# Ending two middle units in phase one, and loading the query weights by pairs of heads on the activation queue

## The reference, cut to what matters

```
p  = rms_norm(x) @ w_in              # 1024 x 2304: q, k, v of two attentions
h  = x + [rms_norm(stick_breaking(q,k,v)), rms_norm(sink_window(q,k,v))] @ w_out
xn = rms_norm(h)
q  = xn @ w_q                        # 1024 x 2048: 8 heads x 2 halves x 128
s1, s2 = q[:,:,0] @ keys_1.T, q[:,:,1] @ keys_2.T
idx, gate = top 16 of the sums of the top 16 of s1 and of s2; gate = softmax
y  = h + sum over 8 heads x 16 experts of gate * gelu(u[idx] . xn) * v[idx]
out = rms_norm(y)
```

## Time and profile before

| | |
|---|---|
| median of three runs | 3066.2 us |
| the profiled execution | 3064.77 us, its span 3063.0 us |
| mean granted TensorE clock | 0.91 of full speed |
| TensorE busy | 2455.0 us (80%) |
| VectorE busy | 2209.8 us (72%) |
| POOL busy | 1530.8 us (50%) |
| ScalarE busy | 1413.2 us (46%) |
| moved by DMA | 1216.86 MB, mean 397 GB/s |
| of it the gathers' queue | 1108.81 MB |

### The profile page before, as it was taken

One profiled execution on the slowest core, in us unless ns is written; L12 is line 12 of the kernel. 1 busy time (PEld: TensorE's weight loads), 2 busy tenths in 40 slices (PEclk: granted clock), 3 DMA queues, 4 the chain that ended last, 5 costly groups with the idle time before them and its releaser, 6 DMA issues.

```text
span 3063.0 us, 44243 instructions
## 1 busy us (share of the span) xinstructions
PE 2455.0 (80%) x13294; PEld 1144.1 (37%) x13294; DVE 2209.8 (72%) x5717; ACT 1413.2 (46%) x3303; POOL 1530.8 (50%) x1597
## 2 busy tenths in 40 slices
PE   7978778787768888878788888888778877778777
PEld 4755334343323332433243323333343334432222
DVE  3278647894667867886788768886878767786886
ACT  2235324652246533753376337753676345643233
POOL 0045444454445555555645565555545555455554
PEclk8999989899879999999989998999999987899989
DMA  8379999999999999999999999999999999999997
GB/s 337 98 281 393 423 394 416 402 404 379 424 419 414 419 418 422 415 408 406 424 419 415 402 416 421 411 409 415 422 414 417 392 420 423 420 402 417 426 422 311
DMA packets 243631, 1216.86 MB, mean 397 GB/s; under 512 B 30528, under 2 KB 90304, under 8 KB 107200
## 3 DMA queue, kind: packets, MB, share of 16 engines
q0 software_dynamic: 152528, 1108.81, 87.4%
q1 hardware_dynamic: 67968, 91.78, 8.4%
q10 hardware_dynamic: 22896, 13.44, 1.4%
HBM read 1197.56 MB, written 16.47 MB: 396 GB/s over the span
## 4 chain that ended last, share of the span: by engine, by line
DMA 34%; PE 24%; DVE 21%; issue 8%; DVEq 5%; ACT 3%; ACTq 1%; POOL 1%; SPq 0%; POOLq 0%
DMA r_uv<-peer_uv,f_idx 31%; DVE r_uv L1222 8%; PE f_y_acc L1769 6%; PE f_z L1654 5%; PE f_q_ps L1695 3%; PE f_y_acc L1750 2%; PE f_y_acc L1621 2%; DMA f_work<-w_out 1%; POOL r_uv L1000 1%; PE f_o_sw L1681 1%; PE f_z L1512 1%; PE f_o_sw L1621 1%; DVE f_ind L1363 1%; ACT f_diag L1146 1%; ACTq L1144 1%
## 5 line engine op out<-in xcount | busy, mean ns | idle before, releaser
L1000 POOL DMA_INDIRECT r_uv<-peer_uv,f_idx x1056 | 1278.5, 1211 | 1188.8 <-PE f_y_acc L1769 818.6
L1222 DVE CUSTOM_DVE_ANT_0 r_uv<-r_uv,r_x_rep 128x1024 f32<-128x1024 f32 x1056 | 1289.4, 1227 | 555.9 <-DMA r_uv<-peer_uv,f_idx 547.5
L1769 PE MATMUL f_y_acc<-r_uv,f_diag 128*32 128x512 f32 x4224 | 678.6, 662 | 330.0 <-ACT f_diag L1146 329.4
L1140 ACT ACTIVATE f_act_hid<-f_hid 128x2 f32<-128x2 f32 x528 | 107.6, 204 | 1087.3 <-DVE f_hid L1222 1084.9
L1750 PE MATMUL f_y_acc<-r_neg_ones,f_zeros 128*32 128x512 f32 x948 | 453.8, 614 | 0.0
L986 POOL TENSOR_TENSOR f_gate_fold<-r_fold,f_gates 128x64 f32<-128x64 f32 x528 | 246.3, 467 | 258.8 <-ACT f_diag L1146 242.8
L1769 PEld LDWEIGHTS f_y_acc<-r_uv,f_diag 128*32 128x32 f32 x4224 | 103.9, 112 | 615.7 <-ACT f_diag L1146 509.0
L1695 PE MATMUL f_q_ps<-r_w_q,f_xnT 128*128 128x256 f32 x1152 | 306.9, 413 | 3.4 <-DVE f_pick L1354 3.4
L1146 ACT ACTIVATE f_diag<-f_gate_fold,f_act_hid 128x32 f32<-128x32 f32 x1056 | 282.1, 314 | 37.8 <-issue 1.4
L1140 ACT ACT_TABLE_LOAD x210 | 269.4, 1283 | 5.3 <-issue 1.6
L1695 PEld LDWEIGHTS f_q_ps<-r_w_q,f_xnT 128*128 128x128 f32 x1152 | 227.3, 205 | 118.6 <-issue 76.9
(11 more groups left out here) (212 smaller groups left out, 3050.0 us busy)
## 6 DMA issues: line engine op xcount, KB each, us to landing
r_uv<-peer_uv,f_idx POOLq DMA_INDIRECT x1056, 13.0
r_w_out<-w_blocks SPq DMA_DIRECT2D x36, 256.0 KB, 8.8
f_work<-out_sb_v_prompt SPq DMA_DIRECT2D x72, 128.0 KB
f_work<-scratch_projT ACTq DMA_DIRECT2D x70, 128.0 KB, 9.7
r_uv<-w_blocks SPq DMA_DIRECT2D x16, 512.0 KB, 11.0
r_w_q<-w_peer_q SPq DMA_DIRECT2D x8, 1024.0 KB, 11.4
x_in<-x_prompt SPq DMA_DIRECT2D x8, 512.0 KB, 10.5
f_q_pad<-scratch_projT SPq DMA_DIRECT2D x64, 64.0 KB, 11.6
```

What stands on the lines that cost most here:

```text
L1000: pool.indirect_dma_start(uv[:, n % RING, :], None, io["peer_uv"], bass.IndirectOffsetOnAxis(ap=idx[:, head, k:k + 1], axis=0),).then_inc( ...
L1140: nc.scalar.activation(act_hid[:, batch % 4, :], hid[:, batch % 8, :], ACT.Gelu)
L1222: nc.vector.tensor_tensor_reduce(row_u, row_u, x_rep[:, g % 3, :], 1.0, 0.0, ALU.mult, ALU.add, hid[:, n // 2 % 8, n % 2:n % 2 + 1]).then_ ...
L1769: last = nc.tensor.matmul(y_acc[quarter, g % 2 * 512:(g % 2 + 1) * 512], diag[:, batch % 3, i, :], uv[:, n % RING, DM + b * 512:DM + (b + ...
```

## The change

1. The last two chunks of tile 0 are blocks 12 to 14 and 15 to 17 instead of 12 to 15 and 16, 17. Blocks 15 to 17 lie in the three buffers of `r.x_rep`, and the second half of `xnT_middle` moves to `r.g_final`. The accumulators of phase one are two banks instead of four, and `y_acc` is allocated for both phases.
2. Middle units 0 and 1 (blocks 4 and 5) are computed at the end of phase one into `y_acc`. The other middle units move in the slots, and late units too.
3. w_q is no longer loaded in phase one but in four DMAs of two heads each (128 partitions x 8 k x 2 KB), issued by ACT after each window pair's exponentials of tile 0. `queries` waits for its own pair of heads.
4. The three first halves of late weights are loaded at slot -23.
5. `q_pad` is cleared in two halves; the first half of q and the first keys are loaded before the second half of q.
6. The orders of ACT, DVE and TensorE in phase one change. The eighth gather waits for 17 units instead of 18.

```diff
-CHUNKS = ((4, 4), (0, 4), (8, 4), (12, 4), (16, 2))
+C_TRIPLE = 15
+CHUNKS = ((4, 4), (0, 4), (8, 4), (12, 3), (C_TRIPLE, 3))
...
-        acc = [ps(f"proj{s}", [P, 4 * P]) for s in range(4)]
+        acc = [ps(f"proj{s}", [P, 4 * P]) for s in range(2)]
...
                 load_x(i)
-                load_w_q(i - 4)
...
-            for k in range(len(ORDER) - 4, DK):
-                load_w_q(k)
-            for p in range(3):
-                load_late(sp, io, r, p)
...
             normalise(4)
+            normalise(5)
             rows_out(2)
-            normalise(5)
             normalise(6)
             rows_out(3)
             normalise(7)
+            normalise(8)
             rows_out(4)
-            normalise(8)
...
+            def middle_unit(u):
+                if u == 0:
+                    pe.wait_ge(s_xnT, T_LATE)
+                for k in range(DK):
+                    last = nc.tensor.matmul(r.y_acc[:, u * 512:u * 512 + MIDDLE], w_blocks_of(r, MIDDLE_ORDER[u], 1)[:, 0, k, :],
+                                            r.xnT_middle[k // 4][:, k % 4, :], start=(k == 0), stop=(k == DK - 1))
+                last.then_inc(r.s_late_mm, 1)
...
             turn_x(2)
             project(2, 0)
+            turn_x(3)
             project(2, 1)
             turn_rows(1)
-            turn_x(3)
+            turn_x(4)
             project(3, 0)
-            turn_x(4)
+            turn_x(5)
             project(3, 1)
-            turn_x(5)
+            turn_x(6)
             project(4, 0)
-            turn_x(6)
+            turn_x(7)
             project(4, 1)
             turn_rows(3)
-            turn_x(7)
             turn_rows(4)
             turn_x(8)
+            for u in range(BORDER_UNITS):
+                middle_unit(u)
...
-MIDDLE_ORDER = [4, 5, 6, 7, 0, 1, 2, 3, 17, 16, 8, 9, 10, 11, 12, 13, 14, 15]
+MIDDLE_ORDER = [4, 5, 6, 7, 0, 1, 2, 3, 15, 16, 8, 9, 10, 11, 12, 13, 14, 17]
-MIDDLE_SLOT = [*(FIRST_SLOT + 8 + 4 * i for i in range(8)), -52, -47, -34, -30, -25, -19, -14, -8, 0, 5]
-LATE_SLOT = [*MIDDLE_SLOT, 10, 18, 22, 26, 32, 42, 50, 54, 58, 62, 66, 70, 76, 82, 87, 92, 100, 105, 109, 114, 131, 145, 155, 160,
-             165, 173, 177, 181, 185, 189, 193, 197, 201, 205, 209, 213]
+MIDDLE_SLOT = [*(FIRST_SLOT + 4 * i for i in range(8)), -60, -54, -47, -34, -28, -17, -11, -5, 1, 11]
+LATE_SLOT = [*MIDDLE_SLOT, 18, 26, 30, 34, 42, 50, 54, 58, 62, 66, 70, 74, 78, 82, 86, 90, 94, 102, 106, 114, 131, 145, 155,
+             160, 165, 173, 177, 181, 185, 189, 193, 197, 201, 205, 209, 213]
...
-X_FIRST = [-10, -5, 12, 60, 98, 126, 168, 188]
+X_FIRST = [-10, -5, 20, 60, 98, 126, 168, 188]
...
                     load_k(sync, *at)
+                    if at == (0, 0):
+                        load_second_q()
...
+                if n == route_slot(0, 0):
+                    for p in range(3):
+                        load_late(sync, io, r, p)
...
-            nc.gpsimd.memset(q_pad[:], 0.0).then_inc(S["zeroed"], 1)
+            for f in range(2):
+                nc.gpsimd.memset(q_pad[:, f, :, :, :], 0.0).then_inc(S["zeroed"], 1)
...
-                    hold(pool, S["late_mm"], 2 * n + (2 if n < RING // 2 else 4))
+                    hold(pool, S["late_mm"], 2 * n + 2 if n < RING // 2 else min(2 * n + 4, N_MIDDLE - 1))
...
+            def load_w_q(two_heads):
+                cols = slice(two_heads * 4 * QH, (two_heads + 1) * 4 * QH)
+                src = io["w_peer_q"].rearrange("(k p) n -> p k n", p=P)
+                act.dma_start(w_q[:, :, cols], src[:, :, cols]).then_inc(r.s_w_q[two_heads], 16)
...
                     window_exp(*at)
+                    if at[0] == 0:
+                        load_w_q(at[1])
...
-                    if m == 0:
-                        pe.wait_ge(r.s_w_q, DK * 16)
+                    if t == 0 and head % 2 == 0:
+                        pe.wait_ge(r.s_w_q[head // 2], 16)
```

More of the change, by code:

```diff
@@ L177, in resident @@
     r.nat_late = late[:, at:at + 2 * PIECE].rearrange("p (s t n) -> p s t n", s=2, n=P)
-    r.s_w_q = ctx.enter_context(nc.semaphore("w_q_loaded"))
+    r.y_acc = ctx.enter_context(nc.psum_tensor("y_acc", [P, DM], F32))
+    r.s_late_mm = ctx.enter_context(nc.semaphore("late_mm"))
+    r.s_w_q = [ctx.enter_context(nc.semaphore(f"w_q_loaded{i}")) for i in range(4)]
     r.s_w_late = [ctx.enter_context(nc.semaphore(f"w_late_loaded{i}")) for i in range(3)]
     return r
+MIDDLE_ORDER = [4, 5, 6, 7, 0, 1, 2, 3, 15, 16, 8, 9, 10, 11, 12, 13, 14, 17]
+BORDER_UNITS = 2
 LATE_ORDER = [0, 1, 2, 3, 4, 5, 6, 7, 8, 9, 10, 11, 17, 16, 12, 13, 14, 15]
-RING_PLACE = {**{c: c - 4 for c in range(4, 8)}, **{c: c + 4 for c in range(4)}, **{c: c for c in range(8, 16)}}
+RING_PLACE = {**{c: c - 4 for c in range(4, 8)}, **{c: c + 4 for c in range(4)}, **{c: c for c in range(8, C_TRIPLE)}}
 def w_blocks_of(r, c, n):
-    if c >= C_KVSW:
-        return r.w_pair[:, c - C_KVSW:c - C_KVSW + n, :, :]
+    if c >= C_TRIPLE:
+        return r.w_triple[:, c - C_TRIPLE:c - C_TRIPLE + n, :, :]
     return r.w_ring[:, RING_PLACE[c]:RING_PLACE[c] + n, :, :]
@@ L213, in projection_phase @@
         x_in = sb("x_in", [P, 4, DM])
-        squares = r.g_final
+        squares = r.w_late[:, 0:2, :, :].rearrange("p s k n -> p (s k n)")
         stat = sb("p1_stat", [P, 4, 6])
@@ L316, in rows_out @@
                 act.wait_ge(s_mm, j + 1)
-                nc.scalar.activation(rows[:, j, 0:n * P], acc[j % 4][:, 0:n * P], ACT.Copy,
-                                     scale=column_scale(c)).then_inc(s_ev, 1)
+                scaled = sum(column_scale(b) != 1 for b in range(c, c + n)) * P
+                if 0 < scaled < n * P:
+                    nc.scalar.activation(rows[:, j, 0:scaled], acc[j % 2][:, 0:scaled], ACT.Copy, scale=SCALE)
+                    last = nc.scalar.activation(rows[:, j, scaled:n * P], acc[j % 2][:, scaled:n * P], ACT.Copy)
+                else:
+                    last = nc.scalar.activation(rows[:, j, 0:n * P], acc[j % 2][:, 0:n * P], ACT.Copy, scale=column_scale(c))
+                last.then_inc(s_ev, 1)
             for i in range(3):
@@ L390, in _ @@
             scale_turned(6)
+            normalise(8)
+            scale_turned(7)
             stage_out(3)
[L392 removed]
             stage_out(4)
[L394 removed]
             scale_turned(8)
@@ L476, in _ @@
                     stores += 1
-                elif c == C_KVSW:
-                    pool.dma_start(io["v_window"][0:P, :], rows[:, j, P:2 * P]).then_inc(s_st, 16)
+                elif c == C_TRIPLE:
+                    pool.dma_start(io["v_window"][0:P, :], rows[:, j, 2 * P:3 * P]).then_inc(s_st, 16)
                     stores += 1
@@ L543 @@
 for u, slot in enumerate(LATE_SLOT):
-    for k in range(DK):
+    for k in range(DK) if u >= BORDER_UNITS else ():
         LATE_K_AT.setdefault(slot + k // 2, []).append((u, k))
@@ L649, in fused_phase @@
         y_stat = sb("y_stat", [P, 6])
-        y_acc = ps("y_acc", [P, DM])
+        y_acc = r.y_acc
         z = ps("z", [P, DM])
@@ L661, in fused_phase @@
                    gate_fold dot diag vmm y_ev y_fold added squares mean guess y_out y_stored copies
-                   late_mm late_w late_ev late_turned late_nat w_first w_out op_w g_final""".split()
+                   late_w late_ev late_turned late_nat w_first w_out op_w g_final""".split()
         S = {n: sem(n) for n in names}
+        S["late_mm"] = r.s_late_mm
         S_UV = [sem(f"uv{i}") for i in range(RING)]
@@ L787, in _ @@
         def _(sync):
-            hold(sync, S["zeroed"], 1)
             def load_q(t, f, chunk):
@@ L804, in load_step_q, with load_second_q @@
                     late_stored(MIDDLE_ORDER.index(C_QSW) if t == 1 else len(UNITS))
-                for f in range(2):
-                    if t:
-                        hold(sync, S["zs"], 4 * t - 2 + 2 * f)
+                for f in range(2 if t else 1):
+                    hold(sync, S["zs"] if t else S["zeroed"], 4 * t - 2 + 2 * f if t else 1)
                     load_q(t, f, 2 * f)
+            def load_second_q():
+                hold(sync, S["zeroed"], 2)
+                load_q(0, 1, 2)
             def load_window_q(t, f, steps):
@@ L913, in stream_w_out @@
                     hold(sync, S["y_out"], t - 1)
+                else:
+                    hold(sync, S["late_mm"], N_MIDDLE)
                 sync.dma_start(w_stream[k % 2], io["w_out"][k * P:(k + 1) * P, :]).then_inc(S_WS[k % 2], 16)
@@ L1114, in copy_x @@
                 if g < 3:
-                    act.wait_ge(S["late_mm"], N_MIDDLE if g == 2 else MIDDLE_ORDER.index(C_KVSW) + 1)
+                    act.wait_ge(S["late_mm"], MIDDLE_ORDER.index(C_TRIPLE + g) + 1)
                 if g >= 3:
```

22 lines of the change are left out of this document (10 added, 12 removed).

## The result

| kernel | median, us | runs | ratio to before, 95% interval |
|---|---|---|---|
| before | 3070.4 | 20 | |
| changed | 3082.0 | 20 | 1.0037 [1.0024, 1.0049] |
| changed, on another occasion | 3084.0 | 12 | 1.0036 [1.0021, 1.0052] |

The change makes the kernel 0.37% slower. The forecast was 3055, with a range from 3047 to 3064. It started from a before of 3066.2, the median of three runs; that of these 20 is 3070.4, so the forecast gain of 11.2 us has to be held against a loss of 11.5, and the sum misses 22.7 us. The profiled execution of the changed kernel took 3094.9 us (its span 3093.1), the slowest of its runs; a second profiled one has a span of 3084.1. Where the two differ, both are told.

What follows compares the result with a forecast made beforehand. From about 200 us the sixteen DMA engines, full with gathers of expert rows, bound the kernel. Gains of 5.4 us at the first gather and 6.8 at the hole, less 1.0, make 11.2: 3066.2 to 3055.0, range 3047 to 3064.

Steps and rivals of the forecast that it cites:

- f: Late units: unit 20's second weight half comes late, PE waits about 9 us, the 290:300 hole grows, 1 us lost.
- a: Border from phase one to the fused phase: first scores at 70.2, 0.6 us later (between -0.4 and +1.5).
- b: First scores to turn of merged: fewer pairs of k, against two latencies that show; net -1.9 us.
- R2: Rival, chance 0.10: query-weight issues hold ACT, each of four windows 2.2 us late, time 3063.8 us.
- c: Product to the turn of xn: eight pairs become six, the chain under it limits the gain; -1.7 us.
- d: Turn of xn to the second head's queries: 13.56 us become 11.1, -2.4 us; first gather at 161.5.
- e: Hole in the gathers at 190: eighth gather waits for one unit less, the hole closes, -6.8 us.
- R3: Rival, chance 0.07: second halves of units 24, 30, 32, 34 come late, PE stops 6.8 us each, 27 us lost, 3082.

Runs made afterwards that it cites:

- Experiment 7: Changed kernel with late units as in the kernel before and query weights loaded in phase one on SP again: 3059.6 us, 0.9949 of before.
- experiment 5: Changed kernel with third and fourth query-weight pairs issued at slots -41 and -37: 3079.2 us, 1.0045; with the old late slots too: 3058.6 and 3054.7 us.
- Experiment 6: Changed kernel with late units as in the kernel before and the eighth gather waiting for all 18 middle units again: 3069.7 us, 0.9974 of before.
- experiment 1: Changed kernel with late units, their banks, last middle unit and third x copy as before: 3056.3 us, 0.9974; second series 3058.5 us, 0.9959.
- experiment 2: Kernel before with only the late units' slots and banks of the changed kernel: 3093.4 us, 1.0089 of before.
- experiment 13: Changed kernel with window loads of tile 1 and later tiles put behind the late half on SP: 3080.4 us, 1.0034 of before.

## Why the prediction was wrong

The step that failed is f, the late units; new holes between 270 and 600 us were among the signs of being wrong that the prediction named. The other steps came out:

- **a, border**: first scores at 70.50 and 70.19 (70.2 said), units done by 64.9 and 65.2 (64.4 said). Right. Experiment 7 shows the price of the late x tile: 3.6 us at the scores.
- **b, to the turn of merged**: 115.94 in the second profile (116.3 by the working), 119.77 in the first. The windows' issues were bounded by 0.66 and 2.47 us; three took 0.37 to 0.44, the fourth 4.29 and 3.97, above the upper end. It cost some 2 us (experiment 5) where the sum had nothing and 0.8 at most, so b came out right by an offset elsewhere: without it the turn comes at 115.14 and 114.93. R2's hold of ACT is real, but for one window, not four; that an issue lasts as long as its transfer is not shown.
- **c, d, first gather**: 161.63 in the second profile, 161.5 said. From the turn of merged to the turn of xn it gained 1.45 us (1.7 said), from there to the first gather 2.26 (2.4 said). The first profile, 165.47, lost its 4 us before 120. Right.
- **e, hole at 190**: closed, the eighth gather at 181.21 (about 180 said) in the second profile, 186.48 in the first. Experiment 6 opens a hole of 10.3 us of the engines' time again; in the timed runs the 6.8 of the step is neither shown nor contradicted.
- **f, late units**: this is the step that failed. It put one wait of 9 us at unit 20 and 1 us of time on it, since five outstanding gathers would keep the DMA engines busy for 14 us. The wait was 11.9 and 12.3 us. And the cover had to last not for the wait but from one gather to the next, 18.5 us: the hole was about 9 us of the engines' time in the first profile (shares 0.71, 0.52 and 0.87 in 270:300) and 10 in the second. Three more waits, which the sum put at nothing, followed at units 32, 34 and 36; behind the last, of 15.2 us, the second hole opened (0.58 in 520:540, 8.4 us). By the ratios of experiments 1 and 2 the late slots cost 19 to 27 us, and 22.7 are missing.
- **R3** had the kind of loss, its price (27 us) and the time, and I gave it 0.07. In part that is luck. Of its four units, 24, 30, 32 and 34, two waited, 32 and 34, and these two waits, 2.1 and 6.1 us, left no hole; the holes came at 20 and 36. Its four equal waits of 6.8 us were 11.9, 2.1, 6.1 and 15.2, and its 3082 starts from a before of 3066, 4 us under that of the 20 runs. Against it I set that three distances of four slots made no wait in before. That was no evidence: with four slots units 24 and 30 did not wait after the change either. What decides is what SP's engine and SP's queue have ahead of the half, and step f had the row for it, a half issued late behind SP's wait for tri that landed in 15.00 us. I used that row for unit 20, and for the rest only the earlier trace rows's landing without asking what it came from.
- R3's mechanism was half wrong. The halves are not slow for the gathers' sake alone: the same load lands in 9 us from ACT's queue beside full gathers, and in 7.3 from SP's when that is empty. They are slow behind other small packets of their own queue.

What stays open: why experiment 13's profile and times differ, what exactly the eighth gather's wait costs, and which step had 2 us to spare in b. A fourth buffer for the halves was not tried for want of room.

## What to carry to other kernels

A load with a deadline must be judged by its whole queue: what the issuing engine waits for ahead of it, and how many packets, not bytes, were issued just before it. When work is moved closer to a prefetch, take the longest issue to landing in the trace as the need, for every such pair and not for the one that stalled before. Whether a stall costs time is read from the distance between two gathers across it, not from its own length. If the slack can't be had, move the load to a queue that is empty at that time before undoing the schedule.

## What the runs showed of the hardware

- Beside saturated gathers SP's queue and the gathers' queue started the same number of packets (869 each in 499:516 of the changed kernel, 397 each in 463.4:471), at 512 bytes a packet in the one and 8 KB in the other. So small packets held up what stood behind them: halves of 256 KB landed 14.07 to 22.87 us after their issue behind 377 to 831 packets, in 7.3 us with SP's queue empty (before, 300:320), and in 9.0 and 9.1 us from ACT's queue.
- The fourth of four 2 MB loads issued on ACT within 12.5 us held it for 4.29 us (3.97 in the second profile, 4.25 in experiment 1), the others for 0.37 to 0.44. The prediction weighed the Trainium skill's "DMA: Bandwidth & Descriptors", Anatomy of one DMA (many descriptors can be emitted before their cost shows). That section describes DMAs issued by GpSimd, and these were issued by ACT: three issues agree with it, and the fourth shows a cost that comes all at once on the engine that issues. What made the fourth slow no run here shows.
- A pause of PE and the hole behind it are not equally long: 11.9 us without work left the DMA engines 9 us short (shares 0.71, 0.52 and 0.87 in 270:300), 15.2 us left 8.4 in 520:540, and 2.1 and 6.1 us left none in 430:510.
